# Expert rows gathered as half rows on 128 partitions, turned by 64x64 products, and down weights read in 8 KB pieces

## The reference

```python
hp = hp + mixer(rms_norm(hp, norm_mix[i]), ...)          # attention
hp = hp + hier_moe(rms_norm(hp, norm_ffn[i]), ...)       # experts

# inside hier_moe, for each frame and each of its two experts e (F = 256):
a = x @ w_gate[e]            # 1024 x 256
u = x @ w_up[e]              # 1024 x 256
y = y + (silu(a) * u * gate) @ w_down[e]   # 256 x 1024
```

## Time and profile before

| | |
|---|---|
| median of 3 runs | 1176.37 us (1175.69 to 1179.66) |
| the profiled execution | 1176.92 us, span 1175.0 us |
| TensorE (PE) busy | 1037.6 us, 88% |
| VectorE (DVE), ScalarE (ACT), GpSimd (POOL) busy | 421.3, 231.9 and 282.9 us |
| DMA over the span | 282.17 MB, mean 240 GB/s |
| weights on queue q1 | 65840 pieces, 240.40 MB, 54.7% of 16 engines |

### The profile page before, as it was taken

How to read it: one execution, slowest core, us unless ns; L and a number is a source line. 1 busy time by engine, 2 the same in 40 slices (tenths; PEclk the granted TensorE clock), 3 DMA queues, 4 the chain that set the end, 5 groups by cost and what they waited for, 6 DMA issues and landing times.

```text
span 1175.0 us, 18007 instructions
## 1 busy us (share of the span) xinstructions
PE 1037.6 (88%) x6864; PEld 738.9 (63%) x6864; DVE 421.3 (36%) x1365; ACT 231.9 (20%) x717; POOL 282.9 (24%) x440
## 2 busy tenths in 40 slices
PE   6999999969999887939899899999997999889970
PEld 6877778955555444528667687777884555555540
DVE  1234454333233222251242533435563333332326
ACT  4234441010000000023122333323310000000001
POOL 3612231022322222122021221221202223221213
PEclk9999999979999999959999999999997999999995
DMA  9312043559999999984320302145176999999996
GB/s 312 112 41 105 8 173 149 192 187 390 371 379 383 377 378 387 403 311 150 108 84 28 127 30 91 64 175 203 41 287 257 385 382 379 376 386 402 376 380 235
DMA packets 82168, 282.17 MB, mean 240 GB/s; under 512 B 10102, under 2 KB 36806, under 8 KB 64352
## 3 DMA queue, kind: packets, MB, share of 16 engines
q1 hardware_dynamic: 65840, 240.40, 54.7%
q0 software_dynamic: 14992, 31.66, 8.3%
q10 hardware_dynamic: 1248, 8.91, 2.0%
HBM read 268.66 MB, written 28.70 MB: 253 GB/s over the span
## 4 chain that ended last, share of the span: by engine, by line
PE 72%; DMA 15%; DVE 4%; SPq 3%; issue 2%; ACT 2%; POOL 1%; ACTq 0%; POOLq 0%; DVEq 0%
PE ps L1767 22%; PE ps L2071 14%; PE ps L1759 10%; DMA area<-in_w_up 9%; PE ps L2083 6%; PE ps L2055 4%; SPq L511 3%; DMA area<-in_w_down 3%; PE ps L2261 2%; PE ps L1743 2%; PE ps L1830 1%; PE ps L1952 1%; PE ps L2227 1%; PE ps L1967 1%; PE ps L1982 1%
## 5 line engine op out<-in xcount | busy, mean ns | idle before, releaser
L1767 PE MATMUL ps<-area 128*128 128x256 f32 x1152 | 267.8, 385 | 7.6 <-DMA area<-in_w_b_qkv 3.9
L2072 PE MATMUL ps<-area 128*64 128x256 f32 x1040 | 252.7, 399 | 0.0
L2071 PE MATMUL ps<-area 128*64 128x256 f32 x912 | 221.6, 399 | 30.2 <-DMA area<-in_w_up 20.3
L1767 PEld LDWEIGHTS ps<-area 128*128 128x128 f32 x1152 | 215.2, 192 | 38.7 <-issue 8.8
L2071 PEld LDWEIGHTS ps<-area 128*64 128x64 f32 x912 | 126.1, 143 | 92.7 <-issue 35.5
L673 POOL DMA_INDIRECT y_scratch<-area,idx_i x64 | 64.8, 1013 | 360.3 <-DVE area L1484 319.7
L2072 PEld LDWEIGHTS ps<-area 128*64 128x64 f32 x1040 | 143.4, 143 | 0.0
L1759 PE MATMUL ps<-area 128*128 128x272 f32 x512 | 123.2, 395 | 0.0
L1469 DVE SCALAR_TENSOR_TENSOR area<-ps,area 64x256 f32<-64x256 f32 x64 | 31.4, 491 | 246.2 <-ACT area L964 246.2
L964 ACT ACTIVATE area<-ps,area 64x256 f32<-64x256 f32 x64 | 29.9, 468 | 449.6 <-PE ps L2072 449.6
L2083 PE MATMUL ps<-area 128*64 128x512 f32 x228 | 109.9, 604 | 1.2 <-DVE area L1477 0.8
(11 more groups left out here) (235 smaller groups left out, 1157.1 us busy)
## 6 DMA issues: line engine op xcount, KB each, us to landing
area<-in_w_up SPq DMA_DIRECT2D x65, 1024.0 KB, 25.5
area<-in_w_gate SPq DMA_DIRECT2D x57, 1024.0 KB, 25.2
area<-in_w_down SPq DMA_DIRECT2D x57, 1024.0 KB, 25.6
area<-in_w_b_qkv SPq DMA_DIRECT2D x12, 1024.0 KB, 8.5
hid<-in_w_down SPq DMA_DIRECT2D x8, 1024.0 KB, 26.3
hid<-in_w_gate SPq DMA_DIRECT2D x8, 1024.0 KB, 26.6
area<-y_scratch ACTq DMA_DIRECT2D x8, 1024.0 KB, 8.1
area<-in_w_a_qkv SPq DMA_DIRECT2D x6, 1024.0 KB, 13.0
```

The source lines that it names most:

```text
L1767: ins = nc.tensor.matmul(ps[:r, bank, at_col:at_col + F], x[:, k, COL[t]:COL[t] + r], w[:, k, :], start=k == k0, stop=k == k1 - 1)
L2071: nc.tensor.matmul(ps[0:CAP, bank, 0:F], x[:, k, :], wg[:, k, :], start=k == 0, stop=k == KD - 1)
L2072: ins = nc.tensor.matmul(ps[CAP:P, bank, 0:F], x[:, k, :], wu[:, k, :], start=k == 0, stop=k == KD - 1)
```

## The change

The residual rows are stored twice, once for each of a frame's two choices, so that `hn_scratch` has the shape of the scatter's target, 4 rows of 512 per frame. The gather then uses the scatter's list: 128 partitions, slot plus 64 x half, of 512 elements. One instruction makes that list. The turn of x becomes 16 products of 64 x 64 with the identity: of each slice k the two halves, which stand in different rows and different columns of the array and write different partitions of one PSUM bank. Down weights are read as one piece of 8 KB per partition (rows 2p and 2p + 1), and the turn of h takes every second element to match.

```diff
-    hn_dram = nc.dram_tensor("hn_scratch", [N, D], F32).ap()
+    hn_dram = nc.dram_tensor("hn_scratch", [4 * N, OUT_HALF], F32).ap()
...
-    c[:, C_HALF] = np.arange(P) // CAP
+    c[:, C_HALF] = 2 * KEY0 + np.arange(P) // CAP
...
-    xg = [part(D * (i // 2), D)[CAP * (i % 2):CAP * (i % 2) + CAP, :] for i in range(XG)]
+    xg = [part(OUT_HALF * i, OUT_HALF) for i in range(XG)]
...
+    def residual_rows(t):
+
+        return hn_dram[4 * COL[t]:4 * COL[t] + 4 * ROWS[t], :].rearrange("(p c h) d -> p c (h d)", c=2, h=2)
...
-        down = [I["w_down"][l].rearrange("g e (c p) d -> (g e) p c d", p=P) for l in range(2)]
+        down = [I["w_down"][l].rearrange("g e (p c) d -> (g e) p c d", p=P) for l in range(2)]
...
-                    sp.dma_start(hid[:, t, :], hn_dram[COL[t]:COL[t] + P, :]).then_inc(tile_in[t], 16)
+                    sp.dma_start(hid[:, t, :], residual_rows(t)[:, 0, :]).then_inc(tile_in[t], 16)
...
-            pool.dma_start(hn_dram[COL[t]:COL[t] + r, :], hid[:r, t, :]).then_inc(y_out[i % 2], 16)
+            pool.dma_start(residual_rows(t), hid[:r, t, :].unsqueeze(1).broadcast_to([r, 2, D])).then_inc(y_out[i % 2], 16)
...
-                                             bass.IndirectOffsetOnAxis(ap=idx_i[0:CAP, 1, e:e + 1], axis=0),
-                                             bounds_check=N - 1, oob_is_err=False).then_inc(gath[e % XG], 16)
+                                             bass.IndirectOffsetOnAxis(ap=idx_i[:, e:e + 1], axis=0),
+                                             bounds_check=4 * N - 1, oob_is_err=False).then_inc(gath[e % XG], 16)
...
-            wait_apart(pool, r_idx, 2 * layer + 1)
+            wait_apart(pool, r_idx, layer + 1)
             for e in range(XG):
                 gather(e)
-            pool.wait_ge(r_idx, 2 * layer + 2)
...
-            own(dve, nc.vector.tensor_scalar(idx_i[:, 2, :], ps[:, 3, 0:NE], -1.0, float(KEY0), ALU.mult, ALU.add))
-            nc.vector.tensor_scalar(idx_i[:, 1, :], idx_i[:, 2, :], 1, None, ALU.arith_shift_right).then_inc(r_idx, 1)
-            own(dve, nc.vector.tensor_scalar(em[:, 0, :], ps[:, 3, 0:NE], -2.0, float(2 * KEY0), ALU.mult, ALU.add))
-            nc.vector.tensor_scalar(idx_i[:, 0, :], em[:, 0, :], cst[:, C_HALF:C_HALF + 1], None, ALU.add) \
+            nc.vector.tensor_scalar(idx_i[:, :], ps[:, 3, 0:NE], -2.0, cst[:, C_HALF:C_HALF + 1], ALU.mult, ALU.add) \
                 .then_inc(r_idx, 1)
...
-                x = xg[e % XG].rearrange("p (c k) -> p k c", k=KD)
-                lo = CAP * (e % 2)
+                turn_rows(xg[e % XG], 2 + b).then_inc(x_flip, 1)
+
+            def turn_rows(rows, bank):
+
+                x = rows.rearrange("p (c k) -> p k c", k=KD)
                 for k in range(KD):
-                    ins = nc.tensor.transpose(ps[:, 2 + b, k * CAP:k * CAP + CAP], x[:, k, :],
-                                              ident[lo:lo + CAP, lo:lo + CAP])
-                ins.then_inc(x_flip, 1)
+                    for lo in (0, CAP):
+                        ins = nc.tensor.matmul(ps[lo:lo + CAP, bank, k * CAP:k * CAP + CAP], x[lo:lo + CAP, k, :],
+                                               ident[lo:lo + CAP, lo:lo + CAP], start=True, stop=True)
+                return ins
...
             def expert_ht(h, bank):
+                rows = h[CAP:P, :].rearrange("s (p c) -> s c p", c=2)
                 for c in range(2):
-                    ins = nc.tensor.transpose(ps[:, bank, c * CAP:c * CAP + CAP], h[CAP:P, c * P:c * P + P],
-                                              ident[CAP:P, CAP:P])
+                    ins = nc.tensor.transpose(ps[:, bank, c * CAP:c * CAP + CAP], rows[:, c, :], ident[CAP:P, CAP:P])
                 return ins
```

More of the change, by code:

```diff
@@ L312, in program @@
     junk = [part(norm_at[n] + 3 * D if n in norm_at else R_G, D) for n in range(5)]
-    xg = [part(D * (i // 2), D)[CAP * (i % 2):CAP * (i % 2) + CAP, :] for i in range(XG)]
-    xg_extra = part(R_G, D)[0:CAP, :]
+    xg = [part(OUT_HALF * i, OUT_HALF) for i in range(XG)]
+    xg_extra = part(R_G, OUT_HALF)
     M1 = XG // 2 * D
@@ L320, in program @@
     hts = [part(M1 + 1536 + 128 * i, 2, CAP) for i in range(2)]
-    yout = [part(M1 + 1792 + 512 * i, OUT_HALF) for i in range(2)] + [part(R_G, OUT_HALF)]
+    yout = [part(M1 + 1792 + 512 * i, OUT_HALF) for i in range(2)] + [part(R_G + OUT_HALF, OUT_HALF)]
     assert M1 + 1792 + 2 * 512 <= slot_at["W0"] and slot_at["W0"] + SLOT <= M0
@@ L349, in program @@
     first_of = sb("first_of", [P, NT, 2, 8], U32)
-    idx_i = sb("idx_i", [P, 3, NE], I32)
+    idx_i = sb("idx_i", [P, NE], I32)
     ov_i = sb("ov_i", [P, 8], I32)
@@ L667, in gather @@
                 nc.gpsimd.indirect_dma_start(xg[e % XG], None, hn_dram,
-                                             bass.IndirectOffsetOnAxis(ap=idx_i[0:CAP, 1, e:e + 1], axis=0),
-                                             bounds_check=N - 1, oob_is_err=False).then_inc(gath[e % XG], 16)
+                                             bass.IndirectOffsetOnAxis(ap=idx_i[:, e:e + 1], axis=0),
+                                             bounds_check=4 * N - 1, oob_is_err=False).then_inc(gath[e % XG], 16)
             def scatter(e):
                 wait_apart(pool, ye_sb, NE * layer + e + 1)
-                nc.gpsimd.indirect_dma_start(y2_dram, bass.IndirectOffsetOnAxis(ap=idx_i[:, 0, e:e + 1], axis=0),
+                nc.gpsimd.indirect_dma_start(y2_dram, bass.IndirectOffsetOnAxis(ap=idx_i[:, e:e + 1], axis=0),
                                              yout[e % 2], None, bounds_check=4 * N - 1, oob_is_err=False) \
@@ L679, in overfull_gather @@
                 nc.gpsimd.indirect_dma_start(x, None, hn_dram,
-                                             bass.IndirectOffsetOnAxis(ap=ov_i[0:CAP, 4:5], axis=0),
-                                             bounds_check=N - 1, oob_is_err=False).then_inc(s["gath"], 16)
+                                             bass.IndirectOffsetOnAxis(ap=ov_i[:, 5:6], axis=0),
+                                             bounds_check=4 * N - 1, oob_is_err=False).then_inc(s["gath"], 16)
             def overfull_scatter(o):
@@ L1484, in y_copy @@
                 nc.vector.tensor_copy(yout[b], ps[:, 6 + b, :]).then_inc(ye_sb, 1)
-            STEPS = 11
+            STEPS = 8
             k = [0]
@@ L1531, in overfull_rows @@
                     op0=ALU.mult, op1=ALU.add, accum_out=ovs[:, 117:118]))
[L1532 to L1535, removed]
+                nc.vector.tensor_scalar(ov_i[:, 5:6], ovs[:, 115:116], -2.0, cst[:, C_HALF:C_HALF + 1], ALU.mult, ALU.add) \
                     .then_inc(s["idx"], 1)
@@ L2118, in overfull_expert @@
                 wait_apart(pe, s["gath"], 16 * (o + 1))
[L2119 to L2122, removed]
+                turn_rows(rows, 3).then_inc(s["xf"], 1)
                 pe.wait_ge(s["xs"], o + 1)
```

## The result

The changed kernel takes 1217.35 us (median of 6 runs, 1216.08 to 1218.24) against 1176.89 us before (6 runs): 1.0338 times as long, with a 95% interval of 1.0324 to 1.0353. The prediction said 1169.5 us and faster; the time is outside its range, and slower instead of faster. The profiled execution has a span of 1216.4 us, 41.4 more than before.

What follows compares the result with a forecast made beforehand. The weight stream through full DMA engines was taken as the bound, TensorE close behind. Layer 0 at -3.95 and layer 1 at -3.0 us, together -7, gave 1169.5 us on the median's scale; range 1161 to 1180.

Steps and rivals of the forecast that it cites:

- 64x64 turns: Turn of x on TensorE: 16 products run as side-by-side pairs, 1.1 us, nothing more than before; one after the other 1.95.
- rival B': Turn of x: partial loss of 0.2 to 0.4 us per expert, such as strided loads; 1174 to 1179 us; chance 0.12.
- signs of being wrong: Down weights and turn of x: a piece price that does not fall, or a turn above 1.3 us.
- rival B: Turn of x: a pair's two tiles run one after the other, +0.86 us per expert; 1211 or 1204 us; chance 0.13.
- The turn of h: Reading every second element on TensorE: +0.1 us per expert, hidden in layer 0 and nearly in layer 1.
- The gain of the stream: DMA in the expert stages: -4.2 for pieces, +0.3 for the gather, -0.15 for the list, per layer.
- a stretch of 1.087: DMA in the expert stage: pieces took 3534 us of engine time where prices from calm stretches make 3250.
- calm prices: DMA engine time per piece in two calm stretches: 163 ns for 4 KB, 311 ns for 8 KB.
- Down weights in 8 KB pieces: Weight stream, the main gain: 3.5 to 7.6 us less per layer, 4.2 taken, near the proportional end.
- Residual rows stored twice: Stores before the first gather: cost 0, covered by 3 us of routing; without that cover 1.9 us per layer.
- The index list: List before each layer's first gather: one instruction replaces two, gather 0.15 to 0.2 us earlier, -0.15 per layer.

Runs made afterwards that it cites:

- experiment 2: Changed kernel with the loops of the turn of x exchanged, all eight slices of the first half, then all of the second: 1361.08 us, 1.1543 of before.
- experiment 1: Changed kernel with each slice of the turn of x taking 128 side-by-side elements instead of every eighth: 1137.29 us, 0.9656 of before.
- experiment 4: Changed kernel with down weights back in two 4 KB pieces and the turn of h over side-by-side elements: 1207.33 us, 1.0246 of before.
- experiments 5 to 7: The first of these: kernel before, but one gather brings two experts' 4 KB rows to 128 partitions: 1195.46 us, 1.0152; experiment 6 and experiment 7 follow.
- experiment 6: Kernel before with one 128-partition gather for two experts, issued one expert earlier in GpSimd's order, ahead of the scatter: 1151.65 us, 0.9786 of before.
- experiment 7: Changed kernel with each gather in two instructions of 64 partitions each: 1217.99 us, 1.0351 of before.
- experiment 3: Kernel before with only down weights in 8 KB pieces and the turn of h by every second element: 1174.90 us, 0.9971 of before.

## Why the prediction was wrong

**The step that failed is the turn of x ("64x64 turns").** It took "a pass of 64 columns is then about 0.054 us" and 16 x 0.054 + 0.22 = 1.1 us for pairs side by side. The pairs were right (experiment 2 shows what their absence costs), the duration was not: it came from L1967 and L1952, whose stationary operands lie side by side, while the turn loads every eighth element. The sum priced a pair by the columns that pass and its loads at nothing. Loads of every eighth element come 0.11 us apart one after the other (3.62 / 32) and 0.13 us apart in pairs (2.14 / 16), which makes the 2.14 us. The sign was in the earlier trace rows, where L2055's strided load takes 201 ns and L2077's contiguous one 137; the prediction used those rows for the turn of h and not for the turn of x, whose loads went from 8 to 32: twice for the halves, and twice because a plain product leaves two records where the transpose left one.

The mechanism does stand in the prediction, as the example of rival B' ("strided loads that no longer fit behind 64-column passes"), but at 0.2 to 0.4 us per expert; it measured 1.05. Two of the prediction's own signs of being wrong or of B and B' came: a turn above 1.3 us, and no waits for weights left in layer 1.

**The time is that of rival B by another mechanism.** B asked for tiles that run one after the other, +0.86 us; what came is +1.05 (2.14 - 1.09) from loads, in pairs. Its sum for the layers was about +10 and +24, with nothing gained by DMA; measured were +11.9 and +28.4. That the two sums are close is luck: a serial pair of passes and a pair of strided loads happen to cost nearly the same. By the prediction's own terms, 31 turns and 32 turns of h at 0.11 make 36 us, less 19.5 of waits 16.6 in layer 0; one turn and one turn of h more, less 7.1, 30.1 in layer 1. That is 6.4 above the measured sum; of this, 5.4 show in the page, where the up products are busy for 247.3 us (L2073, 392 ns each) against 252.7.

The rule that B leaned on, in the Trainium skill, TensorEngine Tiling (Array Packing), Restrictions and Gotchas, is that different row tiles can't use one PSUM bank at once. It does not set the time here. With both row tiles in one bank, on different partitions, 32 passes took 1.15 us in experiment 1, where the prediction's price has 1.7 for passes in turn (32 x 0.054), and in the changed kernel pairs took 2.14 where single ones took 3.62.

**The turn of h** was put at +0.1 us: 0.45 against 0.34, right. It was said to be hidden, and with TensorE the bound it is not: going back to 4 KB pieces and the old turn of h (experiment 4) takes about 10 us off.

**The gain of the stream had its main term missing.** The sum gave the gather +0.3 us per layer, for the number of its pieces. The pieces are not what it costs: while a gather to 64 partitions runs, the rate of all queues together falls (experiments 5 to 7). With only that undone, layer 0 is 16.5 us shorter and layer 1 7.3 (experiment 6). The prediction did see the effect, as "a stretch of 1.087" between the calm prices and the stage, and put it down to the pieces in general. The stage's DMA view (257 to 500, against the earlier trace rows):

```profile
DMA packets 16687, 93.46 MB, mean 385 GB/s; under 512 B 3080, under 2 KB 3080, under 8 KB 6550
...
q1 hardware_dynamic: 11952, 84.94, 85.2%
q0 software_dynamic: 4710, 8.16, 9.1%
```

More bytes in less engine time: 0.852 against 0.909 on q1. By the prediction's calm prices these pieces make 3228 us (10137 of 8 KB and 464 of 4 KB) and took 3312, so the stretch of 1.087 has fallen to 1.03.

The rule that was missed stands in the Trainium skill: SBUF — State Buffer, section "Door 1: The DMA port swizzle (why `[64,N]` ≈ `[32,N]`)", says that DMA bandwidth depends on how many of the 16 memory ports a transfer's partitions reach, and that partitions 0 to 63, or 64 to 127, reach only 8. The dips of experiment 7, to about 300 GB/s from 412, agree with it. That a narrow transfer also slows the wide ones beside it is what these runs add: in the kernel before the weight queue q1 moves 0.42 MB from 304 to 305 us and 0.21 MB from 308 to 309, in a dip. That ports are the reason was not shown here, only that the number of partitions in one instruction decides.

**Down weights in 8 KB pieces** were to be the main gain, 4.2 us per layer of some 250, 1.7%. The count is right: q1 has 57520 pieces over the span instead of 65840, 128 fewer for each of 65 experts. The rate rises by 2 GB/s of 377 with the old gather (0.5%), and by 4 to 7 of 402 to 412 with gathers to 128 partitions (1.0 to 1.7%), each read from one trace: mis-sized for the kernel before, near the proportional end once the dips are gone. In experiment 3, with the turn of h, 2.1 us in layer 0 and nothing in layer 1 were left of it.

**Residual rows stored twice** cost nothing that shows, as said: they land in 4.8 us instead of 3.6, and the gather waits for the list. **The index list** was to bring 0.15 us and brought none that shows: GpSimd's first gather starts 1.53 us after the list instruction (252.15 on VectorE), 1.50 before.

## What to carry to other kernels

Before a turn is cut into smaller products, count its weight loads and price them from a row with the same stride and the same kind of product. Here a load of every eighth element took 212 ns for 64 columns (in a plain product) and 201 for 128 (in a transpose), so four times as many loads cost about twice the time even in pairs. A share of 1.00 on the DMA engines does not say that they move what they can: look at the rate in slices of a microsecond, find what stands at each dip, and let gathers cover all 128 partitions in one instruction. And a gain that moves the bound to another engine by a few microseconds needs that engine's slack counted for every other edit in the change.

## What the runs showed of the hardware

- A stationary load of 64 columns in a plain float32 product takes 137 ns side by side and 212 ns at every eighth element. One of 128 columns in a transpose takes 137 ns side by side, 202 at every second and 201 at every eighth; in plain products, side by side, it takes 186 to 192 (L1952 and L1767 of the kernel before).
- Two row tiles that write different partitions of one PSUM bank run side by side: 2.14 us in pairs, 3.62 in sequence.
- A gather in one instruction to 128 partitions leaves the DMA rate of the stage flat at 412 GB/s; the same bytes in two instructions to 64 partitions each bring it to 384, with dips to about 300.
